# Attention over a prompt on one Trainium2 core: the step at which a pair's query weights are split into two parts

## What is computed

```python
q = (cq @ w_uq).reshape(B, T, N_HEADS, QK_NOPE + QK_ROPE)        # 16 heads, 64 + 32
q_rope = rope(q[..., QK_NOPE:], pos)
s = (einsum('bqhk,bsk->bhqs', qb, ckv) + einsum('bqhr,bsr->bhqs', qrb, kr)) * ATTN_SCALE
s = jnp.where(key_pos[None, :] <= qpos[:, None], s, -jnp.inf)
p = jax.nn.softmax(s, axis=-1)
o = einsum('bhqs,bsk->bqhk', p, ckv)                             # then w_uv and w_o
```

## Time and profile before

| | |
|---|---|
| median of 3 runs | 2711.77 us (2708.47 to 2716.03) |
| the profiled execution | 2707.22 us, of which its span is 2705.1 us |
| TensorE (matmul) busy | 2512.9 us, 93% of the span |
| VectorE busy | 1697.0 us, 63% |
| ScalarE busy | 1276.2 us, 47% |
| GpSimd busy | 321.5 us, 12% |
| TensorE's mean granted clock | 0.974 of full speed |
| chain that ended last | TensorE 50%, VectorE 10%, ScalarE 3% of the span |

### The profile page before, as it was taken

The page is one execution under the profiler, slowest core; times in us unless marked ns, Lnnn a source line. Parts: engine busy times, 40 slices in busy tenths (PEclk is TensorE's granted clock), DMA queues, the critical chain, the costliest instruction groups (busy, mean ns, idle before and its releaser), DMA issues.

```text
span 2705.1 us, 48959 instructions
## 1 busy us (share of the span) xinstructions
PE 2512.9 (93%) x18858; PEld 2286.5 (85%) x18858; DVE 1697.0 (63%) x3281; ACT 1276.2 (47%) x2926; POOL 321.5 (12%) x349
## 2 busy tenths in 40 slices
PE   6786999999979889999999999999999999999995
PEld 2775666666657888999999999999989999999995
DVE  3513555555622357776667885876885877776665
ACT  4322343343411566544446655555554555544443
POOL 0000000000000243000003211302312301200003
PEclk9897999999989989999999999999999999999998
DMA  5102222222364412222222222223222222232221
GB/s 216 43 17 84 90 90 90 90 90 79 115 218 139 177 56 85 79 93 88 87 87 102 79 86 71 79 86 109 99 71 79 87 81 92 87 122 86 93 87 63
DMA packets 70982, 255.10 MB, mean 94 GB/s; under 512 B 7746, under 2 KB 15298, under 8 KB 64354
## 3 DMA queue, kind: packets, MB, share of 16 engines
q1 hardware_dynamic: 70034, 251.27, 26.3%
q10 hardware_dynamic: 720, 0.71, 0.1%
HBM read 244.88 MB, written 7.07 MB: 93 GB/s over the span
## 4 chain that ended last, share of the span: by engine, by line
PE 50%; DVE 10%; ACT 3%; issue 3%; POOL 1%; DMA 0%; POOLq 0%; ACTq 0%; DVEq 0%
PE psum L2461 10%; PE psum L2460 10%; PE psum L2459 10%; PE psum L2434 5%; PE psum L2436 5%; PE psum L2435 5%; DVE t_conv L2295 3%; DVE t_w_lo L2277 2%; DVE t_y L2327 1%; PE psum L2416 1%; PE psum L2418 1%; PE psum L2000 1%; PE psum L2417 1%; DVE t_scaled L1772 1%; POOL t_stat L1926 1%
## 5 line engine op out<-in xcount | busy, mean ns | idle before, releaser
L2459 PE MATMUL psum<-t_h,t_w_hi 128*128 128x272 f32 x2816 | 817.0, 290 | 3.2 <-DVE t_w_lo L2277 3.2
L2461 PE MATMUL psum<-t_h,t_w_lo 128*128 128x272 f32 x2816 | 813.5, 289 | 0.0
L2460 PE MATMUL psum<-t_h,t_w_hi 128*128 128x272 f32 x2816 | 812.4, 288 | 0.0
L2459 PEld LDWEIGHTS psum<-t_h,t_w_hi 128*128 128x128 f32 x2816 | 531.8, 189 | 4.5 <-DVE t_w_lo L2277 3.4
L2460 PEld LDWEIGHTS psum<-t_h,t_w_hi 128*128 128x128 f32 x2816 | 532.1, 189 | 1.1
L2461 PEld LDWEIGHTS psum<-t_h,t_w_lo 128*128 128x128 f32 x2816 | 532.0, 189 | 0.0
L2434 PE MATMUL psum<-t_g_hi,t_w_hi 128*128 128x272 f32 x1408 | 411.2, 292 | 27.8 <-DVE t_w_lo L2277 16.6
L2295 DVE SCALAR_TENSOR_TENSOR t_conv<-t_u,t_taps,t_conv 128x272 f32<-128x272 f32 (+2 forms) x528 | 339.1, 642 | 151.8 <-ACT t_conv L2199 145.6
L2327 DVE TENSOR_TENSOR t_y<-psum,t_y 128x272 f32<-128x272 f32 x640 | 279.5, 437 | 202.6 <-PE psum L2436 198.3
L2435 PE MATMUL psum<-t_g_lo,t_w_hi 128*128 128x272 f32 x1408 | 406.1, 288 | 0.0
L2436 PE MATMUL psum<-t_g_hi,t_w_lo 128*128 128x272 f32 x1408 | 405.5, 288 | 0.0
(11 more groups left out here) (213 smaller groups left out, 3619.6 us busy)
## 6 DMA issues: line engine op xcount, KB each, us to landing
t_raw<-in_ffn_w SPq DMA_DIRECT2D x264, 512.0 KB, 3.5
late_w<-in_ada_late SPq DMA_DIRECT2D x40, 1024.0 KB, 4.8
cache<-in_cache SPq DMA_DIRECT2D x64, 320.0 KB, 4.9
ada_w<-in_ada_w SPq DMA_DIRECT2D x4, 2048.0 KB, 19.5
t_raw<-in_wo SPq DMA_DIRECT2D x16, 512.0 KB, 3.8
pair_raw<-in_pair_w SPq DMA_DIRECT2D x8, 768.0 KB, 6.3
x<-in_x SPq DMA_DIRECT2D x2, 2176.0 KB, 10.7
out_x_out<-x SPq DMA_DIRECT2D x4, 1088.0 KB, 5.9
```

What stands on the lines that cost most here:

```text
L2459: pe.matmul(bank, t.w_hi[s][:, o], hi, start=kt == 0, stop=False)
L2460: pe.matmul(bank, t.w_hi[s][:, o], lo, start=False, stop=False)
L2461: last = pe.matmul(bank, t.w_lo[s][:, o], hi, start=False, stop=kt == KT - 1)
```

## The change

`SPLIT_STEP` is 11. The splits of the query weights for pairs 2 to 7 are issued at step 11 of the pair two places ahead (pairs 0 to 5), on ScalarE behind `first_half` of step 10 and ahead of `exps` of step 12, on VectorE ahead of `maxes` of step 12. They were issued at step 0 of the pair one place ahead (pairs 1 to 6). The split for pair 1 stays at step 0 of pair 0, and that for pair 0 stays ahead of the loop. ScalarE's wait for the jobs is then on those of pair i + 1, which TensorE ends in step 9 of pair i. The number of instructions stays the same on every engine, and TensorE's and SyncE's programs are not edited.

```diff
--- before.py
+++ after.py
@@ -749,6 +749,7 @@
 
 
         LATE_STEP = STEPS - 1 - LATE_A_PAIR
+        SPLIT_STEP = LATE_STEP + 1
 
         def late(jj, b, n):
 
@@ -829,12 +830,14 @@
                     wait(act, late_turned, u)
                     act.activation(late_rows[:], late_out, ACT.Copy).then_inc(late_copied, 1)
 
-            def pair(i, s, turn, jj, b, first=False, last=False):
+            def pair(i, s, jj, b, first=False, last=False):
                 hi, exp = (each_step(i, first, last, *x) for x in ((-1, first_half), (1, exps)))
                 for n in range(STEPS):
                     hi(n)
-                    if n == 0 and not last:
-                        split(i + 1, 1 - s, turn)
+                    if n == 0 and first:
+                        split(1, 1, 16)
+                    if n == SPLIT_STEP and i + 2 < HP:
+                        split(i + 2, s, 16 * (i // 2 + 2))
                     exp(n)
                     copy_late(late(jj, b, n - 1))
                     if n in SLOT_OF_JOB and not last:
@@ -845,11 +848,11 @@
             for j in range(len(JOBS)):
                 job(0, j, 0)
             exps(0, 0, 0)
-            pair(0, 0, 16, -1, 2, first=True)
+            pair(0, 0, -1, 2, first=True)
             for j in range(HP // 2 - 1):
-                pair(2 * j + 1, 1, 16 * j + 32, j, 1)
-                pair(2 * j + 2, 0, 16 * j + 32, j, 2)
-            pair(HP - 1, 1, None, HP // 2 - 1, 1, last=True)
+                pair(2 * j + 1, 1, j, 1)
+                pair(2 * j + 2, 0, j, 2)
+            pair(HP - 1, 1, HP // 2 - 1, 1, last=True)
             first_half(STEPS * HP - 1, HP - 1, STEPS - 1)
 
         @block.vector
@@ -929,8 +932,10 @@
                 most, norm, take, lo = (each_step(i, first, last, *x) for x in
                                         ((1, maxes), (0, normalise), (-2, attended), (-1, second_half)))
                 for n in range(STEPS):
-                    if n == 0 and not last:
-                        split(i + 1, 1 - s)
+                    if n == 0 and first:
+                        split(1, 1)
+                    if n == SPLIT_STEP and i + 2 < HP:
+                        split(i + 2, s)
                     most(n)
                     norm(n)
                     take(n)
```

## The result

The changed kernel takes 2724.22 us, the median of 6 runs (2723.26 to 2729.61), against 2710.76 us before (6 runs, 2707.15 to 2716.03). The ratio is 1.0051, 95% interval 1.004 to 1.0062: slower by half a per cent, 13.5 us. The profiled execution took 2723.91 us, with a span of 2721.9.

The account below looks back on a forecast made before the run. TensorE, busy 61.6 of 66 us a pair, was taken to set the pace. Per pair 3.19 + 1.57 - 2.52 = +2.24 us, times six +13.4 on the median 2711.8, gave 2725.2 us, range 2713 to 2733.

Parts of the forecast that it names:

- The start of a pair: Starts of pairs 1 to 6: without the split, values starts 2.52 us sooner, six times, -15.1 us.
- Step 11 in order: Step 11, six pairs: the splits delay the late copy, so TensorE's turn comes 3.19 us late, +19.1 us.
- its lower bound: Step 11: only ScalarE's 1.05 us would be lost if VectorE's part came off the chain.
- The clock: After TensorE's 2.92 us idle in step 11 the clock falls, 1.57 us in each of six pairs, +9.4 us.
- The first rival: The clock stays at 1.00 after step 11's idle time: +4.0 us, 2715.8, within 0.3%; chance 0.20.
- its half-way case: The clock falls behind step 11's wait in half of the pairs only: +8.7 us, at the border; no own chance.
- The faster rival: Step 11 hides the moved splits in ScalarE's and VectorE's free time: -8.8 us, or -15.1 if nothing is lost; chance 0.08.
- the sum: All six pairs: 3.19 + 1.57 - 2.52 = +2.24 us each, +13.4 us in all, 2725.2 us.

Follow-up runs that it names:

- e4: Changed kernel with VectorE's split moved behind second_half in step 11 and ScalarE's to the end of step 10; 2696.86 us, ratio 0.9943 to the kernel before.
- e3: Changed kernel with only VectorE's split moved within step 11, from ahead of the maximum to behind second_half; 2699.74 us, ratio 0.9953 to the kernel before.
- e6: Changed kernel with the splits of pairs 2 to 7 done again at step 0 of the next pair; 2740.57 us, ratio 1.0105 to the kernel before.
- e10: The changed kernel, unedited, profiled a second time; 2728.60 us in one run.
- e9: The kernel of e6, unedited, profiled a second time; 2741.66 us in one run.
- e5: Changed kernel with 12 extra unused TensorE matmuls a pair in front of turn_late in step 11; 2716.65 us, ratio 1.0024 to the kernel before.

## Why the prediction was right

**The start of a pair** was put at 2.52 us and measured 2.42. The rows of step 1 have `turn` and not `values` behind the job, and gave 0.1 us too early; why was not tried. Six of them in e4, with nothing else lost, are -14.5 us, and e4's -15.5 (0.9943 of 2711, by its interval -20.3 to -10.3) agrees.

**Step 11 in order** was put at 3.19 us with an idle time of 2.92, and measured 3.20 with 2.93. Every link came from a row of its own, and each held to 0.02 us. e3 shows which link is the heavy one: VectorE's split ahead of the maximum, with its wait for ScalarE's part and that part's wait for TensorE's transposes. ScalarE's 1.05 us alone leave TensorE 0.19 us of wait and make a pair 0.47 us longer (64.13 us in e3, 63.66 in e4). That is less than the 1.05 us that the prediction took for its lower bound, as part of ScalarE's work is hidden even there.

**The clock** was put at 1.57 us a pair, in all six. The size was right (1.64 in e6 between two pairs, 68.43 - 66.85 = 1.58 in e10). "In all six" was a choice. The changed kernel's first profile bears it out, but that was partly luck: over the four profiles of e6, e9, e10 and the changed kernel, 18 of 24 idle times of 2.93 us lowered the clock, two of these for twice the time. What decides it in a given pair stays open; the same kernel gave other pairs in e9 than in e6, so it isn't the program alone. The first rival, the clock at 1.00 everywhere, was seen in single pairs, but in none of the four profiles as a whole; its half-way case, a fall in three of six, was seen in e6. Without this term the forecast would have been +4 us, within the 0.3% that the prediction calls no change. e5, which takes only the clock's part away, measures that case at a ratio of 1.0024. So this term decides between no change and slower.

The Trainium skill ("TensorE: Matmul & The Clock Gate", section "Why this matters for your kernels") warns of idle gaps somewhat longer than 2.93 us, and taken at its word lets this one pass. The runs differ from it: 18 of 24 such gaps lowered the clock, and the measurement decides.

**The faster rival** fell: TensorE came 3.20 us late for two instructions of 1.05 and 1.22 us, since the maximum runs only 1.47 us behind the start of VectorE's split. But e4 shows that it was a matter of two places in the program order, not of the idea. The Trainium skill ("Perfetto Trace Analysis", section "Identifying Performance Opportunities") asks to have what blocks the busiest engine start sooner. That gained 14.5 us here (6 x 2.42), and the change lost 28.6 us (14.1 + 14.5) at the place where it put the work.

What the sum did not foresee is small. The two profiled spans differ by 16.8 us. Of these 14.1 lie in the six pairs and 3.0 ahead of them (the first split of the loop starts at 246.1 us in the trace before and at 249.1 in the one after, with the same work ahead of it). Other parts of the kernel differ like this between executions, so the agreement with the median to 1 us is partly luck.

## What to carry to other kernels

An engine that is half idle has its free time in certain places, so put moved work behind the last thing that the busy engine waits for in that step, and ahead of an instruction that itself waits; the average share of idle time says nothing of this. A split over two engines is a chain: its second half waits for the first, which waits for whatever stands ahead of it, and all that is queued behind the second half inherits the sum. When a change gives TensorE one idle time of about 3 us in a piece (2.93 here), add the time at the lower clock behind it to the price, as something that happens often and not always.

## What was unexpected of the hardware

The clock's fall is not a property of the idle time alone. The same wait of 2.93 us, behind the same instructions, lowered the granted clock in 6, 5, 4 and 3 of 6 pairs in four profiles of two kernels. A fall cost 1.6 us here, and 3.2 us where it lasted twice as long (70.05 - 66.85 us in e10). And 24 extra matmul instructions in each of six gaps made the changed kernel 7 us faster in all, because they kept TensorE at its 2.4 GHz level.
